# The last layer's gate projection, split: its second half computed inside the recurrence stage, with one pair of PSUM banks for that stage's transposes

## The reference, cut to what matters

```python
def c_layer(x, xc, mod, mod_c, w_in, w_out, lb_f, lb_b, g_norm, ln_g, ln_b, ctx_out):
    ...
    q, zf, zb, i, g = split_cols(modulate_2(x, shift, scale) @ w_in, widths)
    ...
    o_f, oc_f = hgrn2_direction(q, i, zf, lb_f, qc, ic, zfc, ctx_out, reverse=False)
    o_b, oc_b = hgrn2_direction(q, i, zb, lb_b, qc, ic, zbc, ctx_out, reverse=True)
    y = hgrn2_readout(o_f + o_b, g, g_norm, w_out)
    x_new = layer_norm_2(DEEPNORM_ALPHA * x + gate * y, ln_g, ln_b)

def hgrn2_readout(o, g, g_norm, w_out):
    on = o * lax.rsqrt(jnp.mean(o * o, axis=-1, keepdims=True) + RMS_EPS) * g_norm
    B, H, L, dv = on.shape
    return (on.transpose(0, 2, 1, 3).reshape(B, L, H * dv).astype(g.dtype) * jax.nn.silu(g)) @ w_out
```

## Time and profile before

| | before |
|---|---|
| time, three runs | 1837.62, 1837.65, 1841.71 us, median 1837.65 |
| span of the profiled execution | 1839.8 us (its own time lies among those above) |
| TensorE busy | 1556.3 us, 85% |
| VectorE, ScalarE, GpSimd busy | 820.7 (45%), 371.0 (20%), 193.7 us (11%) |
| projection stage, end of its last matmul | 1736.29 us from the span's start |
| recurrence stage | begins 1737.96, ends 1788.42 us |

### The profile page before, as it was taken

The page is one execution under the profiler, slowest core; times in us unless marked ns, Lnnn a source line. Parts: engine busy times, 40 slices in busy tenths (PEclk is TensorE's granted clock), DMA queues, the critical chain, the costliest instruction groups (busy, mean ns, idle before and its releaser), DMA issues. The chain is left out here.

```text
span 1839.8 us, 19287 instructions
## 1 busy us (share of the span) xinstructions
PE 1556.3 (85%) x7431; PEld 934.0 (51%) x7431; DVE 820.7 (45%) x1532; ACT 371.0 (20%) x702; POOL 193.7 (11%) x282
## 2 busy tenths in 40 slices
PE   4999963689999799476789869999889899999877
PEld 3877762688444444242234324544464457646573
DVE  2344559344344367541211132355673315555554
ACT  3222153111101100110001011100350134532230
POOL 0000027300000000002000000000360001203240
PEclk9799986668999899678889989999999999999988
DMA  9221002210877576569999983342300221131100
GB/s 351 81 92 46 1 1 46 53 25 6 291 249 270 185 274 228 208 253 416 414 366 367 393 324 138 124 149 102 137 1 24 92 91 46 46 116 67 48 23 23
DMA packets 127033, 283.72 MB, mean 154 GB/s; under 512 B 28600, under 2 KB 30936, under 8 KB 121691
## 3 DMA queue, kind: packets, MB, share of 16 engines
q1 hardware_dynamic: 123344, 266.78, 39.7%
q0 software_dynamic: 3600, 15.73, 2.1%
HBM read 312.90 MB, written 4.19 MB: 172 GB/s over the span
## 5 line engine op out<-in xcount | busy, mean ns | idle before, releaser
L2256 PE MATMUL ps<-hT,ring 128*128 128x512 f32 x400 | 175.2, 596 | 0.3 <-issue 0.3
L1312 PE MATMUL ps<-ring,hTx 128*128 128x512 f32 x320 | 140.3, 597 | 1.9 <-PEq L178 1.8
L2256 PEld LDWEIGHTS ps<-hT,ring 128*128 128x128 f32 x400 | 76.3, 192 | 94.9 <-issue 94.7
L2599 PE MATMUL ps<-hT,ring 128*128 128x512 f32 x256 | 111.8, 593 | 3.1 <-PEq L2506 2.8
L299 DVE SCALAR_TENSOR_TENSOR ada_acc<-ring,cact,ada_acc 128x512 f32<-128x512 f32 x154 | 104.1, 746 | 0.5
L1312 PEld LDWEIGHTS ps<-ring,hTx 128*128 128x128 f32 x320 | 61.0, 192 | 78.2 <-issue 78.2
L603 PE MATMUL ps<-hTx,ring 128*128 128x256 f32 x384 | 93.3, 400 | 5.3 <-PEq L178 5.3
L2099 PE MATMUL ps<-ring,hT 128*128 128x512 f32 x192 | 86.6, 611 | 2.7 <-ACT hT L2911 1.4
L603 PEld LDWEIGHTS ps<-hTx,ring 128*128 128x128 f32 x384 | 76.3, 201 | 20.4 <-issue 8.0
L2599 PEld LDWEIGHTS ps<-hT,ring 128*128 128x128 f32 x256 | 47.9, 190 | 61.0 <-issue 61.0
L1845 PE MATMUL ps<-ring,hTx 128*32 128x512 f32 x384 | 54.8, 722 | 26.8 <-DMA ring<-in_expert_w 26.7
(11 more groups left out here) (517 smaller groups left out, 2581.6 us busy)
## 6 DMA issues: line engine op xcount, KB each, us to landing
ring<-in_expert_w SPq DMA_DIRECT2D x24, 2048.0 KB, 14.8
far<-in_expert_w SPq DMA_DIRECT2D x24, 2048.0 KB, 18.0
ring<-in_w_in SPq DMA_DIRECT2D x16, 2048.0 KB, 13.5
ring<-in_ada_w SPq DMA_DIRECT2D x12, 2048.0 KB, 9.2
ring<-in_w_ada SPq DMA_DIRECT2D x12, 2048.0 KB, 8.8
ring<-in_w_in_c SPq DMA_DIRECT2D x10, 2048.0 KB, 7.6
ring<-in_expert_w POOLq DMA_DIRECT2D x32, 512.0 KB
far<-in_expert_w POOLq DMA_DIRECT2D x32, 512.0 KB
```

The lines of the kernel that those rows point to most:

```text
L1312: ins = pe.matmul(ps[:, 2 + i % BANKS], hTx[:, kt, t * P:(t + 1) * P], stream.slot(n)[:, kt], start=(kt == 0), stop=(kt == KT - 1))
L2256: ins = pe.matmul(bank, slot[:, kt, c0:c0 + P], hT[:, kt], start=(kt == 0), stop=(kt == KT - 1))
L2599: ins = pe.matmul(bank, slot[:, kt, j % 4 * P:(j % 4 + 1) * P], hT[:, kt], **edge)
```

## The change

Three things. The two panels of the gate are taken apart in the order of panels: the first stays where it was, the second comes after the input's. In the projection stage two of the four gate pieces are left (`range(TT)`). In the recurrence stage TensorE computes the other two (`gate(t, first, last)`, L2864 of the changed kernel, the matmuls at L2869) into banks 2 and 3: the first whole ahead of the first turn, the second in four quarters of two kt between turns. ScalarE copies them to `sg` (`move_gate`, L2815), and takes their Silu in place at the end of its work (L2838), for which GpSimd's multiplication by the gain now waits. All turns use the one pair of banks 0, 1, so each turn waits until ScalarE has copied the one before (`moved` at m). The output panels are issued from the recurrence stage's queue.

```diff
--- before.py
+++ after.py
@@ -247,20 +247,20 @@
 
         lend = lambda: add(lambda slot: [])
         c_panel = {}
-        for name, at in (("zf", 2), ("q", 0), ("zb", 4), (None, 0), ("g", 8), (None, 0), ("i", 6), (None, 0)):
+        for name, at in (("zf", 2), ("zf", 3), ("q", 0), ("q", 1), ("zb", 4), ("zb", 5), (None, 0),
+                         ("g", 8), ("i", 6), (None, 0), ("i", 7), ("g", 9), (None, 0)):
             if name is None:
                 C_LENT = len(stream.panels)
                 lend()
                 continue
-            c_panel[name] = len(stream.panels)
-            for i in range(2):
-                add_cols(ktp(w["w_in_c_2"][0]), (at + i) * PANEL)
+            c_panel.setdefault(name, []).append(len(stream.panels))
+            add_cols(ktp(w["w_in_c_2"][0]), at * PANEL)
         C_OUT = len(stream.panels)
         for i in range(2):
             add_cols(ktp(w["w_out_c_2"][0]), i * PANEL)
         END = len(stream.panels)
 
-        C_FREED = (c_panel["g"] - 1) // RING
+        C_FREED = (c_panel["g"][0] - 1) // RING
 
 
 
@@ -2533,7 +2533,7 @@
                         ssem(n) for n in ("summed", "q_scaled", "arg", "lexp", "lk", "lq", "level", "put_done"))
                     LN = 2
                     pieces = [("zf", j) for j in range(H)] + [("q", j) for j in range(H)] + [("zb", j) for j in range(H)]
-                    pieces += [("g", j) for j in range(2 * TT)] + [("i", j) for j in range(2 * 2 * TT)]
+                    pieces += [("g", j) for j in range(TT)] + [("i", j) for j in range(2 * 2 * TT)]
                     ZB, I_AT = pieces.index(("zb", 0)), pieces.index(("i", 0))
 
                     on_dve = [n in ("zf", "zb") for n, j in pieces]
@@ -2557,7 +2557,7 @@
                     with nc.Block() as block:
                         @block.sync
                         def _(sp):
-                            stream.issue(sp, END)
+                            stream.issue(sp, C_OUT)
 
                         @block.tensor
                         def _(pe):
@@ -2580,7 +2580,7 @@
                             for i, (name, j) in enumerate(pieces):
                                 of = TT if name == "g" else 4
                                 first_of, last_of = j % of == 0, j % of == of - 1
-                                n = c_panel[name] + j // of
+                                n = c_panel[name][j // of]
                                 if first_of:
                                     pe.wait_ge(*stream.arrive(n))
                                 earlier = [m for m in range(i) if bank_of(m) == bank_of(i)]
@@ -2744,15 +2744,18 @@
                     last = (P - 1, 0)
                     pair = lambda bank: ps[:, bank:bank + 2].rearrange("p b (h c) -> p (b h) c", h=4)
                     head = lambda bank, h: ps[:, bank + h // 4, h % 4 * P:(h % 4 + 1) * P]
-                    turn_bank, state_bank, out_bank = (lambda m: m % 2 * 2), (lambda d: 4 + 2 * d), (lambda d: 2 * d)
+                    TURN_BANK, GATE_BANK = 0, 2
+                    state_bank, out_bank = (lambda d: 4 + 2 * d), (lambda d: 2 * d)
                     ssem = stage_sems(scope, "rec_")
                     ks_arg, ks_exp, ks_done, turned, moved, dn_done, s_done, state_done, q_exp, q_near, q_far, o_done, o_added = (ssem(n) for n in (
                         "ks_arg", "ks_exp", "ks_done", "turned", "moved", "dn_done", "s_done", "state_done", "q_exp", "q_near", "q_far", "o_done", "o_added"))
-                    gn_loaded = ssem("gn_loaded")
+                    gn_loaded, gate_proj, gate_moved, gate_silued = (ssem(n) for n in ("gn_loaded", "gate_proj", "gate_moved", "gate_silued"))
+                    late_gate = lambda t: sg[:, t, PANEL:]
                     with nc.Block() as block:
                         @block.sync
                         def _(sp):
                             sp.dma_start(gn[:, :], row_bcast(w["gnorm_c_2"][0])).then_inc(gn_loaded, 16)
+                            stream.issue(sp, END)
 
                         @block.vector
                         def _(dve):
@@ -2807,7 +2810,11 @@
 
                             def move(m):
                                 act.wait_ge(turned, m + 1)
-                                act.copy(keys(m), pair(turn_bank(m))).then_inc(moved, 1)
+                                act.copy(keys(m), pair(TURN_BANK)).then_inc(moved, 1)
+
+                            def move_gate(t):
+                                act.wait_ge(gate_proj, t + 1)
+                                act.copy(late_gate(t), ps[:, GATE_BANK + t]).then_inc(gate_moved, 1)
 
                             def decay_queries(step, d):
                                 act.wait_ge(dn_done, KEYS)
@@ -2815,15 +2822,20 @@
 
                             decay(0)
                             decay(1)
+                            move_gate(0)
                             for m in range(2, KEYS):
                                 move(m - 2)
                                 decay(m)
+                            move_gate(1)
                             decay_queries(TT, 0)
                             decay_queries(TT, 1)
                             move(KEYS - 2)
                             move(KEYS - 1)
                             decay_queries(TT + 1, 0)
                             decay_queries(TT + 1, 1)
+                            act.wait_ge(gate_moved, TT)
+                            for t in range(TT):
+                                act.activation(late_gate(t), late_gate(t), ACT.Silu).then_inc(gate_silued, 1)
 
                         @block.gpsimd
                         def _(pool):
@@ -2835,6 +2847,7 @@
                                 pool.wait_ge(q_exp, 2 + d + 1)
                                 pool.tensor_tensor(part, part, qT[:, :, (tile_at(TT + 1, d) - TT) * P:(tile_at(TT + 1, d) - TT + 1) * P], ALU.mult).then_inc(q_far, 1)
                             pool.wait_ge(gn_loaded, 16)
+                            pool.wait_ge(gate_silued, TT)
                             for t in range(TT):
                                 g = sg[:, t].rearrange("p (h c) -> p h c", h=H)
                                 pool.tensor_tensor(g, g, gn[:, :].unsqueeze(1).to_broadcast([P, H, P]), ALU.mult)
@@ -2843,10 +2856,22 @@
                         def _(pe):
                             def turn(m):
                                 pe.wait_ge(ks_done, m + 1)
-                                if m >= 2:
-                                    pe.wait_ge(moved, m - 1)
-                                transpose_in(pe, turn_bank(m), lambda i: ksf[m % 4][:, i], 4)
-                                transpose_in(pe, turn_bank(m) + 1, lambda i: ksf[m % 4][:, 4 + i], 4).then_inc(turned, 1)
+                                if m:
+                                    pe.wait_ge(moved, m)
+                                transpose_in(pe, TURN_BANK, lambda i: ksf[m % 4][:, i], 4)
+                                transpose_in(pe, TURN_BANK + 1, lambda i: ksf[m % 4][:, 4 + i], 4).then_inc(turned, 1)
+
+                            def gate(t, first, last):
+                                n = c_panel["g"][1]
+                                if t == 0 and first == 0:
+                                    pe.wait_ge(*stream.arrive(n))
+                                for kt in range(first, last):
+                                    ins = pe.matmul(ps[:, GATE_BANK + t], hT[:, kt, L + t * P:L + (t + 1) * P], stream.slot(n)[:, kt],
+                                                    start=(kt == 0), stop=(kt == KT - 1))
+                                if last == KT:
+                                    ins.then_inc(gate_proj, 1)
+                                    if t == TT - 1:
+                                        stream.free(pe, n)
 
                             def add_keys(step):
                                 for d in DIRS:
@@ -2862,6 +2887,7 @@
                                 for d in DIRS:
                                     if step == TT:
                                         pe.wait_ge(moved, KEYS)
+                                        pe.wait_ge(gate_moved, TT)
                                         pe.wait_ge(q_near, d + 1)
                                     else:
                                         pe.wait_ge(o_added, d + 1)
@@ -2873,12 +2899,19 @@
                                         ins = pe.matmul(head(out_bank(d), h), scT[d][x - TT][:, h], vtok[:, x, h * P:(h + 1) * P], start=False, stop=True)
                                     ins.then_inc(o_done, 1)
 
+                            gate(0, 0, KT)
                             turn(0)
+                            gate(1, 0, 2)
                             turn(1)
-                            for step in range(TT):
-                                add_keys(step)
-                                turn(2 * step + 2)
-                                turn(2 * step + 3)
+                            gate(1, 2, 4)
```

(8 more changed lines are left out.)

## The result

The changed kernel takes 1826.2 us in the median of four runs (1825.75 to 1828.16); the kernel before, with a fourth run, 1839.68 us (1837.62 to 1847.14). The ratio is 0.9918 with a 95% interval of 0.9899 to 0.9936: faster, by 13.5 us or 0.8%. The profiled execution is the one of 1825.75 us.

A forecast was written before the change was run, and what follows sets the result against it. TensorE bounds the projection stage; a chain across VectorE, ScalarE, GpSimd and TensorE paces the recurrence stage. -14.2 + 1.1 - 1.6 = -14.7 us, from the median 1837.65 to 1823.0 us, range 1819.5 to 1828.5.

The forecast's parts named there:

- Two go: -14.2 us.: Projection stage: two of four gate pieces, 7.10 us each on TensorE, leave with hidden Silus; the stage ends 14.2 us earlier.
- That leaves 8 us of slack.: Projection stage: GpSimd's product, ready about 1646, precedes the second block of scores at 1654.7, so lost cover costs nothing.
- The panels and the late Silus: Both stages: panel loads land before use, and GpSimd's gains after the late Silus, at about t = 35, stay hidden.
- Outputs start at 29.8, +1.1 us.: Recurrence stage: the outputs' first row at 29.8 us from the stage's start instead of 28.7, costing 1.1 us.
- The gate work fills the 7.4 us in which the clock had fallen, and the full clock pays for the delay.: Recurrence stage's start: turn(0) comes about 1.3 us later, but add_keys(0) ends at t = 16.0 against 16.5 before.
- I take the clock as kept: -1.6 us.: Recurrence stage's outputs: TensorE stays at full clock, so they take 7.2 us instead of 8.8, saving 1.6 us.
- rival 1: Recurrence stage: the clock still falls before the outputs; price +1.6 us, sum -13.1, 1824.6 us; chance 0.22.
- The rule that transposes do not count as activity: Rule set against the forecast, on TensorE's clock in the recurrence stage: by it the sum would be -13.1 us, not -14.7.
- Rival 2: Recurrence stage: the single pair of banks costs at every turn, five waits of 1.2 us, +6.0, 1829.0 us; chance 0.10.
- rival 4: Recurrence stage: not faster; all 14.0 us moved and five bank waits on the pacing chain, +5.8, 1843.5 us; chance 0.06.
- The rule of rotating banks: Rule set against the forecast: independent matmul groups should rotate through PSUM banks; by it the sum would be -8.7 us.
- Rival 3: Recurrence stage: TensorE at low clock when late gate work begins, 6.8 us lost, 1829.8 us; chance 0.08.

## Why the prediction was right, and where it was off

The forecast was 1823.0 us in a range of 1819.5 to 1828.5; 1826.2 was measured. The change of -14.7 us stands against -13.5, for two errors of opposite sign: the outputs started 0.4 us earlier than forecast, and the 1.6 us from the clock did not come. The other 2 us of the difference come from the base: the three runs had a median of 1837.65, and with a fourth it is 1839.68.

- *"Two go: -14.2 us."* Measured -14.22.
- *"That leaves 8 us of slack."* 8.2 by the trace for GpSimd, whose product it was worked out for. The mask that VectorE has to finish for the second half of the scores was left out; it has 6.5 us. With the other half moved as well, 14.2 us less of cover, the first wait was for GpSimd and the second for VectorE, 5.9 us in all.
- The panels and the late Silus were hidden, as forecast. The late gate's first row waited for no transfer, and GpSimd's gains came at t = 35.0 (forecast: about 35):

```profile
1721.54 21.15 SPq L154 DMA_DIRECT2D ring<-in_w_out_c  x2
1756.18 4.67 POOL L2853 TENSOR_TENSOR csg<-csg,cgn 128x1024 f32<-128x1024 f32 x2
```

- *"Outputs start at 29.8, +1.1 us."* 29.4, +0.66. The schedule held row by row (first turn at t = 6.94, add_keys(0) at 12.1, turn (3) at 18.3, add_keys(1) at 21.3), and TensorE's own way, put at 29.6, is what set the outputs. VectorE's way was put too late by 1.8 us: it took 3.20 us for the two queries, not 4.05, and began on them at t = 22.9, not 23.7. The forecast's 29.8 also lay 0.1 us ahead of its own 29.9 for VectorE, which made no difference.
- *"The gate work fills the 7.4 us in which the clock had fallen, and the full clock pays for the delay."* Two runs put a size to it. A filler as long as the first late piece, in the kernel before, brings the outputs from 28.7 to 26.1: this piece pays for itself with 2.6 us to spare. The second piece and the single pair cost 3.3 us (29.4 against 26.1). 14 us were moved for 0.7 us.
- *"I take the clock as kept: -1.6 us."* This step failed: the clock fell as the outputs started, they took 8.87 us, and rival 1 (-13.1 us) is what happened. I had put it at 0.22. The measured time could not have told the two apart, since the range holds both 1823.0 and 1824.6; the rows did. The error was to set idle times of 1.2 to 1.4 us against one of 3.28 and to look at the longest alone: between turn (4) and the outputs TensorE idled 1.19 us, worked 1.07 and idled 1.10. Executions with this same stretch differ: three of the changed kernel fell, the two with another edit elsewhere did not. With the waits filled (two kernels) or with only one of 1.42 us (one kernel) it stayed.
- The rule that transposes do not count as activity (the Trainium skill, TensorE: Matmul & The Clock Gate, Part 4) pointed to the right rival for a reason that this case refutes: 64 transposes of float32 held the full clock for 7 us (one execution; the page measured bf16). So the transposes ahead of the outputs do not explain by themselves why the clock fell.
- Rival 2, the wait at every turn, did not come about: one wait of 1.19 us, and 1.1 us back when it is removed. (The idle time of 11.65 us that rival 4 was set against left out 1.32 us ahead of turn (1) and 0.23 ahead of add_keys(1).) The rule of rotating banks (the Trainium skill, Perfetto Trace Analysis, Matmuls) holds where nothing else fills the copy: with the gate ahead of all turns, turns (1) and (5) waited 1.19 us each for a copy. The gate quarters between the turns are what made one pair enough. Rival 3 (low clock from the start) did not occur, and rival 4 neither: the outputs started at t = 29.4, not behind 42.9.

What stays open: why the clock fell in all three executions of the changed kernel and in neither of the two with the same stretch behind another edit. Five executions do not tell chance from a cause, and no run varied that alone.

## What to carry to other kernels

Work moved out of a stage that one engine fills into the waits of another stage is worth its whole time where it leaves, and costs only what of it lands on the chain where it arrives; cost both by rows, and ask in the first stage what it had covered, on every engine that feeds the next consumer, since a second helping of the same move can take the gain back. Place such filler where a step waits for another, not ahead of them all. Here the first late piece stood ahead of the first turn in every variant; with the second in quarters between the turns the outputs started 3.3 us later than with nearly all of both left out, with it ahead of the turns 7.1 us later, and laid into the waits 1.6 us later. And where a filler keeps TensorE busy in what was idle time, the clock is part of its price, with a value of its own (2.6 us here).

## What the runs showed of the hardware that I had not expected

- float32 transposes kept TensorE's clock up as matmuls did: 64 of them in 7.18 us with a granted clock of 1.00, and the first turn behind them in 1.04 us; with 32 matmuls of 128 columns in 7.38 us it was the same. One execution of each.
- The clock can fall though no single idle time is long: idle times of 1.19 and 1.10 us around one turn of 1.07 were all that stood before the fall in three executions, and in two others it did not fall behind the same rows.
